# Recurrence with early shifts of r and k, gates stored raw with their sigmoids taken in the branches, and weight splits behind a step's work

## What is computed

```python
# each layer of the first block
mix = jax.nn.sigmoid(gate_a) * (o_a @ w_branch_a) + jax.nn.sigmoid(gate_b) * (o_b @ w_branch_b)
return mix @ w_out
...
# the second block
y_attn = chunked_band_attention(...)
y_rwkv, v_first = rwkv7_time_mix(...)
mixed = (gate_a * (y_attn @ w_branch_attn[i]) + gate_b * (y_rwkv @ w_branch_rwkv[i])) @ w_out[i]
```

```python
cols = cols + (prev - cols) * mu                  # the token shift
r, k, v, wd, ad, gd = jnp.split(cols, splits, axis=-1)
decay = jnp.exp(-jnp.exp(w_log)); a = jax.nn.sigmoid(aaa_base + ad @ aaa_up)
kk = heads(k * k_k); kk = kk * lax.rsqrt(jnp.maximum(jnp.sum(kk * kk, -1, keepdims=True), 1e-24))
k = k * (1.0 + (a - 1.0) * k_a)
state = state * wt + sa[..., None] * bt + vt[..., None] * kt      # one step of the scan
...
bonus = jnp.sum(r_h * k_h * r_k, -1, keepdims=True) * v_h
```

## Time and profile before

| | us |
|---|---|
| median of 3 runs | 3024.78 (3020.69 to 3028.4) |
| the profiled execution | 3027.41 |
| its span, first to last instruction | 3026.1 |
| TensorE busy | 2744.8 (91%) |
| VectorE busy | 1659.7 (55%) |
| ScalarE busy | 1227.2 (41%) |
| mean granted TensorE clock | 0.940 |

### The profile page before, as it was taken

The page is one execution under the profiler, slowest core; times in us unless marked ns, Lnnn a source line. Parts: engine busy times, 40 slices in busy tenths (PEclk is TensorE's granted clock), DMA queues, the critical chain, the costliest instruction groups (busy, mean ns, idle before and its releaser), DMA issues.

```text
span 3026.1 us, 36544 instructions
## 1 busy us (share of the span) xinstructions
PE 2744.8 (91%) x14868; PEld 2052.7 (68%) x14868; DVE 1659.7 (55%) x2746; ACT 1227.2 (41%) x1800; POOL 118.8 (4%) x101
## 2 busy tenths in 40 slices
PE   6988899999998997889999999988989989689986
PEld 5766667888877775668788876666666668344445
DVE  3596445545445487545645455345443525477767
ACT  2217743423333225753424233244322312267765
POOL 0010000000000010000000000000000000022210
PEclk9999999999999899999999999899989889789998
DMA  3111232222221121223222222312111033389982
GB/s 116 64 62 63 79 110 91 98 98 97 90 91 60 56 70 60 77 74 132 84 98 98 98 85 82 112 41 79 43 45 66 23 119 125 141 295 392 382 335 97
DMA packets 64139, 334.93 MB, mean 111 GB/s; under 512 B 9568, under 2 KB 10336, under 8 KB 31072
## 3 DMA queue, kind: packets, MB, share of 16 engines
q1 hardware_dynamic: 58848, 324.14, 29.7%
q0 software_dynamic: 5120, 8.40, 0.9%
HBM read 312.58 MB, written 28.31 MB: 113 GB/s over the span
## 4 chain that ended last, share of the span: by engine, by line
PE 76%; DVE 11%; ACT 5%; DMA 4%; issue 3%; SPq 0%; POOL 0%; POOLq 0%; DVEq 0%; ACTq 0%
PE bank L888 14%; PE bank L890 14%; PE bank L889 14%; PE bank L1076 3%; PE bank L1077 2%; PE bank L1078 2%; PE bank L2274 2%; DMA hT<-in_WE 2%; ACT wh L1858 1%; DVE wl L1327 1%; PE bank L1120 1%; PE bank L2997 1%; PE bank L1148 1%; PE bank L1140 1%; PE bank L2983 1%
## 5 line engine op out<-in xcount | busy, mean ns | idle before, releaser
L888 PE MATMUL bank<-XH,wh 128*128 128x512 f32 x1312 | 528.6, 403 | 15.5 <-DVE XL L1368 11.5
L889 PE MATMUL bank<-XL,wh 128*128 128x512 f32 x1312 | 518.1, 395 | 0.0
L890 PE MATMUL bank<-XH,wl 128*128 128x512 f32 x1312 | 517.4, 394 | 0.0
L1327 DVE TENSOR_TENSOR wl<-raw,wh 128x2048 fp32r<-128x2048 f32 (+1 forms) x168 | 371.8, 2215 | 221.3 <-ACT wh L1858 221.1
L1858 ACT ACTIVATE wh<-raw 128x2048 fp32r<-128x2048 f32 (+1 forms) x168 | 309.0, 1842 | 190.0 <-DMA raw<-in_W 187.9
L888 PEld LDWEIGHTS bank<-XH,wh 128*128 128x128 f32 x1312 | 250.5, 191 | 93.9 <-issue 20.2
L890 PEld LDWEIGHTS bank<-XH,wl 128*128 128x128 f32 x1312 | 250.8, 191 | 53.6
L889 PEld LDWEIGHTS bank<-XL,wh 128*128 128x128 f32 x1312 | 251.1, 191 | 52.1 <-issue 2.4
L888 PE MATMUL bank<-arena_rounded,wh 128*128 128x512 f32 x576 | 231.1, 401 | 5.3 <-DVE arena_rounded L1572 3.2
L890 PE MATMUL bank<-arena_rounded,wl 128*128 128x512 f32 x576 | 230.0, 399 | 0.0
L889 PE MATMUL bank<-arena_rounded,wh 128*128 128x512 f32 x576 | 229.7, 399 | 0.0
(11 more groups left out here) (488 smaller groups left out, 4663.3 us busy)
## 6 DMA issues: line engine op xcount, KB each, us to landing
raw<-in_W SPq DMA_DIRECT2D x153, 1024.0 KB, 4.8
arena<-in_WE SPq DMA_DIRECT2D x56, 1024.0 KB, 9.9
hT<-in_WE SPq DMA_DIRECT2D x26, 1024.0 KB, 9.9
cst<-in_WE SPq DMA_DIRECT2D x14, 1024.0 KB, 10.0
gsave<-scr SPq DMA_DIRECT2D x48, 256.0 KB, 2.6
scr<-gsave SPq DMA_DIRECT2D x48, 256.0 KB, 3.9
raw<-in_W SPq DMA_DIRECT2D x8, 768.0 KB, 4.3
arena<-ytok SPq DMA_DIRECT2D x8, 512.0 KB, 7.4
```

The lines of the kernel that those rows point to most:

```text
L888: pe.matmul(ps[0:c.stop - c.start, :], h[:, k, c], hi, start=i == 0, stop=False)
L889: pe.matmul(ps[0:c.stop - c.start, :], h[:, k, c], lo, start=False, stop=False)
L890: mm = pe.matmul(ps[0:c.stop - c.start, :], l[:, k, c], hi, start=False, stop=i == len(xs) - 1)
L1327: w_lo.inc(dve.tensor_tensor(wl[:, i % 3, 0:k], raw[:, i % 3, 0:k], wh[:, i % 3, 0:k].bitcast(F32), ALU.subtract), i)
```

## The change

Three things change, on three engines.

1. **Early shifts.** The shifts of r and k, with kk's product and its square, leave `prep` for a third generator `fresh` that runs in steps 0 to 5 of a stage (r in step 2, k in step 4, the square in step 5); in stage 0 it runs ahead of all steps. In `prep`, TensorE's sum of squares follows the low-rank products in the same step, the reciprocal comes ahead of three VectorE operations, and the bonus product has a step and a wait for S2 of its own; its VectorE part moves behind the scaled copies. The memset of the state moves with the shift of r.
2. **Raw gates.** `gate` copies a tile (Copy in place of Sigmoid). In `branches` ScalarE takes each gate's sigmoid in place in `GB` after its read (`gates_on`), one tile ahead, and VectorE waits for that instead of for the read.
3. **Splits behind a step's work.** In attention ScalarE's `cuts_to` stands behind the exponential and the turned copy of the step; VectorE's stands one step later and behind the normalization. In the recurrence both stand behind `behind`, `fresh` and `ahead` of the step, VectorE's one step later.

```diff
@@ pa and pv: the order of the events follows; gate_on is a new signal
@@ VectorE, attention
-                    for n in cuts_at(m, s):
-                        cuts_to(n)
                     if s < len(todo):
...
                     if 0 <= s - 1 < len(todo):
                         normalize(m, s - 1)
+                    for n in cuts_at(m, s - 1):
+                        cuts_to(n)
@@ VectorE, branches
-                    dve.wait_ge(*gate_r[4 * (j % 2) + i]((m, j, i)))
+                    dve.wait_ge(*gate_on((m, t, 0)))
...
-                    dve.wait_ge(*gate_r[4 * (j % 2) + 2 + i]((m, j, 2 + i)))
+                    dve.wait_ge(*gate_on((m, t, 1)))
@@ ScalarE, gate
-                bank.emptied(act.activation(gate_at(m, g), bank.ap(key), ACT.Sigmoid), key)
+                bank.emptied(act.activation(gate_at(m, g), bank.ap(key), ACT.Copy), key)
@@ ScalarE, attention
-                    for n in cuts_at(m, s):
-                        cuts_to(n)
                     if s < len(todo):
...
                         bank.emptied(act.activation(PT[(s - 2) % 2][:, 0:n], bank.ap(key)[:, 0:n], ACT.Copy), key)
+                    for n in cuts_at(m, s):
+                        cuts_to(n)
@@ ScalarE, branches
+            def gates_on(m, t):
+                j, i = divmod(t, 2)
+                for which in range(2):
+                    x = 2 * which + i
+                    act.wait_ge(*gate_r[4 * (j % 2) + x]((m, j, x)))
+                    s = GB[4 * (j % 2) + x]
+                    gate_on.inc(act.activation(s, s, ACT.Sigmoid), (m, t, which))
             def branches(m, n0):
+                gates_on(m, 0)
                 for t in range(8):
+                    if t < 7:
+                        gates_on(m, t + 1)
                     if t % 2:
                         cuts_to(n0 + t // 2 + 2)
                     high((("mix", m), t), t, MX[t % 2], mixed_o((m, t)))
@@ TensorE, prep
                     bank.filled(mm, (name, j))
-                yield
                 ps = opened(("kksum", j))
...
                 spread_heads(("kkspread", j), ..., pv(("krec", j)))
+                yield
                 ps = opened(("bonus", j))
+                pe.wait_ge(*pv(("s2", j)))
                 mm = pe.matmul(ps, C("blk"), S2, start=True, stop=True)
@@ ScalarE, recurrence
+            def fresh(j):
+                ...
+                yield
+                yield
+                shifted(p.rT, ("rkv", j, 0), j, ("r", j))
+                yield
+                yield
+                shifted(p.kT, ("rkv", j, 1), 4 + j, ("k", j))
+                yield
+                act.wait_ge(*pv(("kkT", j)))
+                pa.inc(act.activation(KSQ, p.kkT, ACT.Square), ("ksq", j))
+                yield
             def prep(j):
                 p = places[j]
-                for i, (dst, x) in enumerate(((p.rT, "r"), (p.kT, "k"), (p.vT, "v"))):
-                    shifted(dst, ("rkv", j, i), 4 * i + j, (x, j))
+                shifted(p.vT, ("rkv", j, 2), 8 + j, ("v", j))
                 for name, dst, base in (("lowd", p.lw, "dbase"), ("lowa", p.aT, "abase")):
...
                 for k in range(STEPS[stage]):
+                    next(behind, None)
+                    next(first, None)
+                    if stage in (0, 4) or k >= 6:
+                        next(ahead, None)
                     if 0 < stage < 4 and k in (2, 7):
                         cuts_to(rk_block(stage) + k // 4 + 2)
                     for b in gate_blocks_half(stage, k):
                         cuts_to(gate_block(b) + 2)
-                    next(behind, None)
-                    if stage in (0, 4) or k >= 6:
-                        next(ahead, None)
@@ VectorE, recurrence
+            def fresh(j):
+                p = places[j]
+                yield
+                yield
+                shifted(p.rT, ("rkv", j, 0), j, ("r", j))
+                v.inc(dve.memset(p.st, 0.0))
+                yield
+                yield
+                shifted(p.kT, ("rkv", j, 1), 4 + j, ("k", j))
+                dve.wait_ge(*bank.empty(("rkv", j, 1)))
+                pv.inc(dve.tensor_scalar(p.kkT, p.kT, K("kk", j), None, ALU.mult), ("kkT", j))
+                yield
             def prep(j):
                 p = places[j]
+                shifted(p.vT, ("rkv", j, 2), 8 + j, ("v", j))
+                dve.wait_ge(*bank.full(("kksum", j)))
+                bank.emptied(dve.tensor_scalar(p.kcols, ..., 1e-24, None, ALU.max), ("kksum", j))
...
                 yield
+                dve.wait_ge(*pa(("kroot", j)))
+                pv.inc(dve.reciprocal(p.kcols, p.kcols), ("krec", j))
...
                 for k in range(STEPS[stage]):
-                    if 0 < stage < 4 and k in (2, 7):
-                        cuts_to(rk_block(stage) + k // 4 + 2)
-                    for b in gate_blocks_half(stage, k):
-                        cuts_to(gate_block(b) + 2)
                     next(behind, None)
+                    next(first, None)
                     if stage in (0, 4) or k >= 6:
                         next(ahead, None)
+                    if 0 < stage < 4 and k in (3, 8):
+                        cuts_to(rk_block(stage) + (k - 1) // 4 + 2)
+                    for b in gate_blocks_half(stage, k - 1):
+                        cuts_to(gate_block(b) + 2)
+                for b in gate_blocks_half(stage, STEPS[stage] - 1):
+                    cuts_to(gate_block(b) + 2)
```

More of the change, by code:

```diff
@@ L592, in program @@
         gate_r = [Signal(sem(f"gate_r{i}"), [(m, j, i % 4) for m in range(3) for j in range(i // 4, 4, 2)], 16) for i in range(8)]
+        gate_on = Signal(sem("gate_on"), [(m, t, which) for m in range(3) for t in range(8) for which in range(2)])
         troot = Signal(sem("troot"), [(li, ti) for li in layers for ti in range(4)])
@@ L2534, in scalar_recurrence @@
                 behind = scan(stage - 1) if stage else iter(())
+                first = fresh(stage) if stage < 4 else iter(())
                 if stage == 0:
                     cuts_to(rk_block(0) + 2)
+                    for _ in first:
+                        pass
                 for k in range(STEPS[stage]):
+                    next(behind, None)
+                    next(first, None)
+                    if stage in (0, 4) or k >= 6:
+                        next(ahead, None)
                     if 0 < stage < 4 and k in (2, 7):
@@ L2584, in prep @@
                 yield
-                dve.wait_ge(*bank.full(("kksum", j)))
-                bank.emptied(dve.tensor_scalar(p.kcols, bank.ap(("kksum", j))[:, 0:8], 1e-24, None, ALU.max), ("kksum", j))
+                dve.wait_ge(*pa(("kroot", j)))
+                pv.inc(dve.reciprocal(p.kcols, p.kcols), ("krec", j))
                 dve.wait_ge(*bank.empty(("lowa", j)))
@@ L2593, in prep @@
                        ("s2", j))
-                dve.wait_ge(*pa(("kroot", j)))
-                pv.inc(dve.reciprocal(p.kcols, p.kcols), ("krec", j))
                 yield
@@ L2607, in prep @@
                                                 op0=ALU.mult, op1=ALU.mult), ("A", j))
-                key = ("bonus", j)
-                dve.wait_ge(*bank.full(key))
-                bank.emptied(dve.tensor_tensor(p.BV, bank.ap(key), p.vT, ALU.mult), key)
                 dve.wait_ge(*pa(("e3", j)))
@@ L2620, in prep @@
                 pv.inc(dve.tensor_tensor(p.kT, p.kT, E3, ALU.mult), ("kT3", j))
+                key = ("bonus", j)
+                dve.wait_ge(*bank.full(key))
+                bank.emptied(dve.tensor_tensor(p.BV, bank.ap(key), p.vT, ALU.mult), key)
                 yield
```

15 lines of the change are left out of this document (6 added, 9 removed).

## The result

The changed kernel takes 2957.02 us (median of 4 runs, 2952.76 to 2970.24) against 3026.59 for the kernel before, run beside it (4 runs). The ratio is 0.978 with a 95% interval of 0.9762 to 0.9799: 69.6 us less, where 58 were forecast. The profiled execution has a span of 2951.4 us and a mean granted clock of 0.948 (before: 0.940). First the page: the busy time of the engines, the chain that ended last by engine, and the split's group.

A forecast was written before the change was run, and what follows sets the result against it. TensorE held 76% of the chain that ended last, so only its pauses and lower clock counted. Attention 32 and 7, recurrence 12, 4 and 4, less 1 for the branches made 58 us: 2967 us forecast, range 2940 to 2998.

The forecast's parts named there:

- both engines have the split at the head of a step: Attention: ScalarE's copy (1.92 us) and VectorE's subtraction (2.29) precede a ready score's reduction; TensorE waits 2.75 us.
- Attention, 32 forecast: Layers 0 and 1: moved splits and raw gates save 16 us each, 12.5 of pauses and 3.5 of clock; bounds 0 and 22.
- over the layer I take back 3.5 us: Attention of layers 0 and 1: gain from a higher clock with fewer pauses, 3.5 us a layer.
- I let 2.7 of them stay as smaller pauses: Attention of layers 0 and 1, L1140: of 10.4 us hanging on splits 2.7 stay, so 7.7 go.
- The Trainium skill's drain: Table loads: the skill page's 1380 ns drain beside each 1283 ns load would put the attention estimate some 5 us higher.
- The third attention, 7 forecast: Third layer's attention: 5.5 us of 8.8 in pauses go, plus 1.5 of clock; bounds 0 and 12.
- The recurrence, 20 forecast: Recurrence: 4 us a stage in stages 1 to 3, 12 in all, 4 in stage 0 and 4 in stage 4.
- I leave its wait as it is (1.9 us): Recurrence, stages 1 to 3: TensorE's wait for the reciprocal L2595 stays at 1.9 us after the early shifts.
- (a): Rival: attention's split pause is put off one step, not removed; 31 us less in all, 2994; chance 0.14.
- (b): Rival: every pause behind a split goes, and the clock with it; 76 us less, 2949; chance 0.12.
- (c): Rival: nothing measurable; recurrence chain is VectorE's own, new load eats its gain, attention's pause put off; 9 less, 3016; chance 0.05.
- (d): Rival: slower; each of 19 attention splits stops TensorE for 4.2 us, deciding from 3.4; 15 more, 3040; chance 0.05.

The follow-up runs named there:

- 2: On the kernel before, all splits of both engines moved behind a step's work in attention and recurrence, gates and shifts as before: 2964.48 us, ratio 0.9797.
- 6: On the kernel before, only VectorE's split in attention moved, behind the normalization and one step later; ScalarE's left at the step's head: 2972.36 us, one execution.
- 10: On the kernel before, VectorE's splits alone moved, in attention and recurrence; ScalarE's splits, gates and shifts as before: 2963.59 us, ratio 0.9802.
- 1: On the kernel before, only the raw gates, with their sigmoids in the branches: 3028.71 us, ratio 1.0012.
- 11: On the kernel before, VectorE's splits alone moved, and the top-k search taken in 2 parts a step instead of 5: 2955.29 us, ratio 0.9766.
- 12: On the kernel before, VectorE's splits moved, top-k search in 2 parts a step instead of 5, and raw gates with sigmoids in the branches: 2952.35 us, ratio 0.9767.
- 3: On the kernel before, only the early shifts of r and k and the new preparation order, splits and gates as before: 3023.15 us, ratio 0.999.
- 5: The changed kernel without its early shifts, preparation in the old order, gates and splits as changed: 2961.74 us, ratio 0.9774.
- 7: On the kernel before, both engines' splits in attention moved behind the step's work, VectorE's in the same step instead of one later: 2988.3 us, one execution.
- 4: On the kernel before, both engines' splits moved in attention only, the recurrence as before: 2985.02 us, ratio 0.9872.

## Why the prediction came out right, and where it didn't

**The cause was the one named.** Splits alone give 61.6 of 69.6 us (2). The prediction's "both engines have the split at the head of a step" named one engine too many for the attentions: VectorE's place costs nearly everything there (6), ScalarE's nothing, and moving ScalarE's takes some 3 us an attention back (182.5 to 185.9), which the gates' missing loads then restore and more (180.9). In the recurrence ScalarE's place costs pauses too (5.4 us at the square, 2 against 10), with no difference in the medians.

**Attention, 32 forecast, 41.5 measured.** By term, a layer: L1140 7.7 forecast, 9.2 measured (12.0 to 2.8); the reduction 3.5 against 1.9 (5.9 to 4.0), but the first steps' pauses under "issue" fell by 1.9 as well (7.6 to 5.7), which the sum didn't have; L934 1.3 against 1.9 (2.9 to 1.0). That is 14.9 against 12.5. The clock is the rest, 5.7 against 3.5. It is granted at 0.97 over the stretch instead of 0.94, as forecast, and 180.9 us is below the 186 expected. Mis-sized most was the clock ("over the layer I take back 3.5 us"), then the first steps' pauses, and then the term "I let 2.7 of them stay as smaller pauses": 1.2 stayed.

**The loads' share was put in the wrong place.** The prediction counted the 1.3 us at L934 for the gates' load; alone it came (2.9 to 1.5) and the attention was 2 us longer all the same (1). On top of the splits the gates give 5 us a layer (185.9 to 180.9), or 1.7 where ScalarE's copies stay at the head (11 to 12). So in attention the parts don't add. In the totals 61.6 for the splits, 2.9 for the shifts and 2.6 lost for the gates make 61.9 alone, against 69.6 together, but the intervals of the splits' kernel alone are 7 us to either side.

**The Trainium skill's drain** (ScalarE: Activation LUTs, "What ACT_TABLE_LOAD costs"), weighed in the prediction as 5 us more for the attention part: the trace doesn't agree. In kernel 6 a gate's load starts at 1268.47, 0.02 us behind the end of the copy ahead of it, and ends at 1269.75; the activation behind it starts at 1269.76. Of the change's 46.5 us on ScalarE, 57 loads of 1.283 us less the 27.9 of sigmoids account for all but 1.3. No run here shows a drain of 1380 ns.

**The third attention, 7 forecast, 8.8 measured.** The wait for the turned copy went from 8.4 in 5 pauses to 4.0 in 4, and one of 2.0 under "issue" left. The clock there is 1.00 instead of 0.96.

**The recurrence, 20 forecast, 19.5 measured, for other reasons.** Stages 1 to 3 were forecast at 12 from the early shifts and gave 4.6. The shifts alone give nothing (3), and on top of the splits nothing is shown (5). The step that failed is "I leave its wait as it is (1.9 us)": the reciprocal's wait became 3.2 in each of these stages in the changed kernel and 4.6 with the shifts alone. The number does come some 6 us earlier in the stage, but TensorE asks for it 9 us earlier (3). Stage by stage, counted from the first product of each stage's r tile, the change gave 5.2 us in stage 0 (4 forecast), then 3.5 lost, 3.5 and 4.6 gained in stages 1, 2 and 3 (4 forecast for each). The kernels of equal recurrence agree within 0.3 us in stages 0 and 1, but not in 2 and 3 (91.2 to 94.4 and 90.8 to 93.9), so only the first two differences are more than such kernels show among themselves. L2314's pause of 4.1 in stage 0 went as said, one of 1.8 at the doubling (L2681) took part of its place, and a new one of 2.6 for the tile K (L2647) came in stage 1; why stage 1 as a whole got longer stays open.

The last stage gave 9.7 for 4. Its two pauses of 3.7 us in all went. The other 6.0 are TensorE's busy time, 55.10 us instead of 61.09 for the same products, at a granted clock of 0.88 instead of 0.80. Of the eight kernels that move VectorE's splits in the recurrence, seven have 59.6 or 59.7 us there and one, kernel 2, has 72.7; the six that don't have 64.9 to 71.9. So the splits make the short stage likely and don't secure it, and the gain that the clock made up there is in part luck; what else decides it stays open.

**The branches, 1 us charged.** The stretch from them to the end has 550.5 us after and 547.9 before, over all kernels 545.4 to 551.5. The sigmoids took 620 ns each (630 forecast), 27.9 us in all; the prediction's 32 for 48 of 0.63 is a slip, it makes 30. Whether they cost anything is below what these runs can tell: the gates alone have a ratio of 0.9999 to 1.0026, nothing to 8 us slower for the whole kernel.

**The rivals.** (a), the pause put off by a step, would have shown pauses of 2 us and more at the turned copies; the longest is 1.2 (1.5 in the third attention), and in kernel 7 one sees VectorE's side of it. (b), that every pause behind a split and its clock goes, named 76 less, and the measured 69.6 lies nearer to it than to the main case's 58; in attention it was nearly right with 50.3 of 56, and its "one cause" is what 6 shows. (c) was right that the early shifts alone would gain nothing, but not that the splits wouldn't pay; whether the chain is VectorE's own isn't shown. (d), a stop of 3.4 us or more a split, didn't come; its sum takes 21 for the recurrence and the branches, where the prediction's own terms make 19. The pauses at the value products were to stay under 1 us, and one of 1.2 is left. The loads came out as listed: none at the gates, one a layer in the branches; three at the decay's sigmoid instead of four.

## What to carry to other kernels

Where two in-order engines handle one job in turn, look at the second one's instruction first. At the head of a step it did harm here, because its wait and its work both stood ahead of short, urgent ones; behind the step's work and one step after the first one's it gave nearly the whole gain. In attention the first engine's could stay where it was. In the recurrence moving it as well took pauses away, so that is to be tried place by place. Before removing work from an engine, see whether TensorE's waits name that work: 33 us of table loads an attention, and a square made earlier, gave nothing of their own here. A part that gives nothing alone can still pay on top of another, as the raw gates did (nothing alone, 5 us an attention with the splits moved), so parts are to be tried together too.

## What was not expected of the hardware

With the pauses goes a lower clock, and the work that was done at 1.2 GHz gives back over a third as much again: in attention 14.9 us of pauses brought 20.6, and the other 5.7 are TensorE's busy time, 165.71 us instead of 171.49. The recurrence's last stage is the reverse case. Its clock differs between kernels whose instructions there are the same (64.9 us at 0.86 in 7, 69.3 at 0.80 in 4, 6 and the kernel before), while the attentions repeat to 0.3 in all kernels but one. So a gain of 10 us read from one stretch of one profile can't be counted on, unless its pauses in the trace account for it; that holds for 6.0 of the change's own 9.7 us in this stage.
